# Softmax biases as negated minima, the sink as a column, and 64x64 products dealt over four corners of TensorE

## The reference, cut to what matters

```
# layer 0: 8 dense heads, and 8 window heads (|i-j| <= 128) with a sink
s = where(valid, q @ k.T * scale, NEG)
p = softmax(concatenate([s, sink_col], axis=-1))[..., :-1];  o = p @ v
# layer 1: 8 latent heads, and 8 neighbourhood heads with a bias
s = where(valid, q @ k.T * scale + bias[h], NEG);  o = softmax(s) @ v
# cross attention: 4 heads of 128 (layers 0 and 1), 4 heads of 256 (second block)
k, v = split(m @ w_kv);  q = h @ w_q
o = softmax(q @ k.T * scale) @ v;  out = o @ w_o
# second block, RWKV-7: 8 heads of 64, token by token
sa = S @ -kk;  S = S * w + outer(sa, kk * a) + outer(v, k);  y = S @ r
# second block, GLA: 4 heads, chunks of 64 tokens
att = where(lower triangle, q_dec @ k_inv.T, 0)
o = att @ v + q_dec @ S;  S = exp(dec) * S + k_dec.T @ v
```

## Time and profile before

| | |
|---|---|
| median of 3 runs | 2944.58 us (2944.35 to 2946.43) |
| the profiled execution | 2944.98 us, span 2943.7 us |
| PE busy | 2873.0 us (98%), 14792 matmuls |
| VectorE busy | 1631.0 us (55%) |
| ScalarE busy | 657.2 us (22%) |
| POOL busy | 0.3 us |
| mean granted TensorE clock | 0.995 of full speed |

### The profile page before, as it was taken

One profiled execution on the slowest core, in us unless ns is written; L12 is line 12 of the kernel. 1 busy time (PEld: TensorE's weight loads), 2 busy tenths in 40 slices (PEclk: granted clock), 3 DMA queues, 4 the chain that ended last, 5 costly groups with the idle time before them and its releaser, 6 DMA issues.

```text
span 2943.7 us, 36398 instructions
## 1 busy us (share of the span) xinstructions
PE 2873.0 (98%) x14792; PEld 1974.0 (67%) x14792; DVE 1631.0 (55%) x3300; ACT 657.2 (22%) x1367; POOL 0.3 (0%) x5
## 2 busy tenths in 40 slices
PE   8999999999999999999999999999999999999998
PEld 3557488888544574888885445455554865688886
DVE  5685644453336855566746983445442633666654
ACT  5651310000136513100000021422220102222200
POOL 0000000000000000000000000000000000000000
PEclk9999999999999999999999999999999999999999
DMA  4013122222211131222221111211112331222222
GB/s 145 29 50 101 51 93 86 86 93 101 79 60 50 68 110 65 91 75 86 86 100 65 52 56 58 72 45 45 45 44 80 120 108 43 72 86 87 91 95 79
DMA packets 61942, 224.26 MB, mean 76 GB/s; under 512 B 6992, under 2 KB 7248, under 8 KB 61264
## 3 DMA queue, kind: packets, MB, share of 16 engines
q1 hardware_dynamic: 61776, 221.94, 22.4%
HBM read 219.82 MB, written 2.10 MB: 75 GB/s over the span
## 4 chain that ended last, share of the span: by engine, by line
PE 92%; DVE 7%; issue 1%; DMA 0%; ACT 0%; SPq 0%; DVEq 0%; ACTq 0%
PE ps L1596 28%; PE ps L647 17%; PE ps L1058 15%; PE ps L1046 8%; PE ps L1111 4%; PE ps L1384 2%; PE ps L1357 2%; PE ps L1073 2%; PE ps L1369 2%; PE ps L2278 1%; PE ps L2753 1%; PE ps L2062 1%; PE ps L2083 1%; DVE probs L1487 1%; DVE shaped L1463 1%
## 5 line engine op out<-in xcount | busy, mean ns | idle before, releaser
L1058 PE MATMUL ps<-h,ring 128*128 128x512 f32 x784 | 361.9, 605 | 0.0
L1596 PE MATMUL ps<-h,ring 128*128 128x256 f32 x1136 | 271.0, 382 | 8.5 <-DVE u L1618 4.6
L1058 PEld LDWEIGHTS ps<-h,ring 128*128 128x128 f32 x784 | 142.7, 190 | 158.7 <-issue 152.6
L1596 PEld LDWEIGHTS ps<-h,ring 128*128 128x128 f32 x1136 | 215.9, 191 | 44.0 <-issue 8.7
L1596 PE MATMUL ps<-h_sums,w_sums 128*128 128x256 f32 x1008 | 224.4, 379 | 0.0
L1596 PEld LDWEIGHTS ps<-h_sums,w_sums 128*128 128x128 f32 x1008 | 191.5, 190 | 26.0
L647 PE MATMUL ps<-hid_sums,d_sums 128*128 128x256 f32 x720 | 171.2, 379 | 1.0 <-DVE hid_sums L1555 1.0
L647 PEld LDWEIGHTS ps<-hid_sums,d_sums 128*128 128x128 f32 x720 | 136.6, 190 | 20.2 <-issue 1.8
L1537 DVE TENSOR_TENSOR d_sums<-ring 128x512 f32<-128x512 f32 (+1 forms) x48 | 31.5, 655 | 171.8 <-DMA ring<-stream_dram 146.7
L1369 PEld LDWEIGHTS ps<-constants,probs 128*128 128x128 f32 x560 | 62.7, 141 | 79.2 <-DVE probs L1487 60.0
L1111 PE MATMUL ps<-o_x,ring 128*128 128x512 f32 x256 | 112.2, 593 | 0.0
(11 more groups left out here) (608 smaller groups left out, 4782.2 us busy)
## 6 DMA issues: line engine op xcount, KB each, us to landing
ring<-stream_dram SPq DMA_DIRECT2D x395, 512.0 KB, 3.6
bias<-bias_dram SPq DMA_DIRECT2D x8, 448.0 KB, 4.5
mem<-mem_dram SPq DMA_DIRECT2D x3, 1024.0 KB, 4.8
x<-x_dram SPq DMA_DIRECT2D x4, 512.0 KB, 8.1
out_dram<-x SPq DMA_DIRECT2D x8, 256.0 KB, 2.2
rope_ab<-ropes_dram SPq DMA_DIRECT2D x4, 256.0 KB, 8.3
s_big<-s_big_dram SPq DMA_DIRECT2D x1, 1024.0 KB, 7.0
constants<-constants_dram SPq DMA_DIRECT2D x1, 768.0 KB, 11.3
```

The source lines that it names most:

```text
L1058: mm = pe.matmul(out, w, r, start=(k == 0), stop=(k == len(rhs) - 1))
L1596: mm = pe.matmul(ps[:, bank + at, 0:256], w(k), x(k), start=start and k == 0, stop=k == 3, skip_group_check=not start)
```

## The change

It has five parts.

1. **Window and bias heads.** tensor_tensor_reduce scales by the negated factor and takes a minimum, which is written directly where ScalarE reads its bias; ScalarE then scales by -1. The negation at L1472 goes for them. The negated sink is the first value of that minimum; POOL copies it into one more column of `shaped` (16 copies of 128x2), and the exponential over w+1 columns sums it. L1471, L1436 and L1482 go.
2. **Cross attention, maxima.** The keys are scaled in the copy that takes them out of PSUM, and one tensor_reduce with negation gives the bias.
3. **Cross attention, start.** The last pair's copy and two adds move into the attention's loops: the copy to ScalarE's step 2, the adds to VectorE's steps 2 and 3. TensorE waits for the adds only ahead of the first values. The attention's buffers move to another address (92 or 124 KB).
4. **RWKV.** The scores and the set of L2359 run with c outside and j inside, and two sets (`r_mvp`, `r_tt`) become one loop that alternates them, at the place of the second.
5. **GLA.** The scores alternate two heads. The masked scores of two chunks form a block-diagonal matrix of 128x128 for each head (zeros once by a POOL memset of 128x2048), and one product per two chunks takes the place of two. The mask becomes eight VectorE instructions on 64 partitions. The set starts at time 31.5, not 30.

The diff, cut to what the text speaks of:

```diff
                 for n in range(nh):
                     act.wait_ge(*s['k_p'].at(n + 1))
-                    act.activation(k[:, n, :], ps[:, n % 4, 0:MEM], ACT.Copy).then_inc(*s['k_out'].up())
+                    act.activation(k[:, n, :], ps[:, n % 4, 0:MEM], ACT.Copy, scale=groups[0].scale).then_inc(*s['k_out'].up())
                 for j, b in enumerate(v_banks):
...
                     self.copy_first(act, i, p1[:, :], bank(i))
-                    act.wait_ge(*s['w_p'].at(7 * i + (5 if i else 2)))
-                    act.activation(q[:, 2 * i, lo], ps[:, bank(i), lo], ACT.Copy).then_inc(*s['w_c11'].up())
+                    if i < n_pairs - 1:
+                        act.wait_ge(*s['w_p'].at(7 * i + (5 if i else 2)))
+                    if i < n_pairs - 1:
+                        act.activation(q[:, 2 * i, lo], ps[:, bank(i), lo], ACT.Copy).then_inc(*s['w_c11'].up())
 
             @block.vector
...
+                    if i < n_pairs - 1:
+                        self.combine_last(dve, i, u[:, :], q[:, 2 * i + 1, lo], q[:, 2 * i, hi], bank(i))
 
...
+        def late_act(act):
+            act.wait_ge(*made[0])
+            act.activation(q[:, nh - 2, lo], ps[:, b, lo], ACT.Copy).then_inc(*s['w_c11'].up())
+
+        def late_dve(dve, part):
+            if part == 0:
+                dve.wait_ge(*v_done)
+            dve.wait_ge(*made[part + 1])
+            dst = (q[:, nh - 1, lo], q[:, nh - 2, hi])[part]
+            dve.tensor_tensor(dst, u[:, :], ps[:, b + 2 + part, 0:256], ALU.add).then_inc(*s['w_c'].up())
+        return late_act, late_dve
...
@@ -1340,6 +1359,21 @@
             def width(u):
                 k0, k1 = span(u)
                 return (k1 - k0) * P
+
+            @block.gpsimd
+            def _(pool):
+                done = 0
+                for u, (p, qt) in enumerate(units):
+                    gr = groups[p]
+                    if gr.sink is None:
+                        continue
+                    if not done:
+                        pool.wait_ge(*s['copied'].at(sum(gr.sink is not None for gr in groups)))
+                    if shaped[u - 2]:
+                        pool.wait_ge(*s['exped'].at(u - 1))
+                    w, at = width(u), 2 * sum(gr.sink is not None for gr in groups[:p])
+                    pool.tensor_copy(sb[:, u % 2, :, w], ns[:, at:at + 2]).then_inc(*s['pool'].up())
+                    done += 1
 
             @block.tensor
...
                     if i == 2 and evac is None:
-                        for done in self.q_done:
-                            pe.wait_ge(*done)
+                        pe.wait_ge(*self.q_done[0])
                     if i == 2 and evac and evac.early:
                         pe.wait_ge(*evac.done(False))
                     if 0 <= i - 2 < n:
                         turn(i - 2)
                     p, part = divmod(i - 6, 4)
+                    if late and p == 0 and part == 0:
+                        pe.wait_ge(*self.q_done[1])
                     if evac and p == 0 and part == 0:
                         pe.wait_ge(*evac.done(True))
                     if p >= 0:
...
                         for j in range(g):
                             src = sb[:, i % 2, j, 0:w] if shaped[i] else ps[:, bank(i, j), 0:w]
                             ins = act.activation(pr[:, i % 3, j, 0:w], src, ACT.Exp, bias=stat_of(i, 1, j),
-                                                 scale=1.0 if shaped[i] else gr.scale, accum_out=stat_of(i, 2, j))
+                                                 scale=-1.0 if shaped[i] else 1.0 if gr.folded else gr.scale,
+                                                 accum_out=stat_of(i, 2, j))
                         ins.then_inc(*s['exped'].up())
-                        if gr.sink is not None:
-                            act.activation(stat(i, 5), stat(i, 4), ACT.Exp).then_inc(*s['act'].up())
...
                             a = (6 - 2 * qt) * GRID
                             add = bs[:, gr.bias[j] % 4, a:a + w] if gr.bias else gr.mask(qt)
-                            first = gr.sink[:, j:j + 1] if gr.sink is not None else NEG
-                            dve.tensor_tensor_reduce(sb[:, u % 2, j, 0:w], src, add, gr.scale, first, ALU.add, ALU.max,
-                                                     stat_of(u, 0, j)).then_inc(*s['biased' if j == g - 1 else 'vec'].up())
+                            first = -NEG
+                            if gr.sink is not None:
+                                at = 2 * sum(gr.sink is not None for gr in groups[:p])
+                                first = ns[:, at + j:at + j + 1]
+                            dve.tensor_tensor_reduce(sb[:, u % 2, j, 0:w], src, add, -gr.scale, first, ALU.add, ALU.min,
+                                                     stat_of(u, 1, j)).then_inc(*s['maxed' if j == g - 1 else 'vec'].up())
+                        elif gr.folded:
+                            dve.tensor_reduce(stat_of(u, 1, j), src, AX.X, ALU.max,
+                                              negate=True).then_inc(*s['maxed' if j == g - 1 else 'vec'].up())
                         else:
                             dve.reduce_max(stat_of(u, 0, j), src, AX.X).then_inc(*s['vec'].up())
+                    if shaped[u] or gr.folded:
+                        return
                     dve.wait_ge(*s['vec'].now())
-                    if shaped[u]:
-                        dve.wait_ge(*s['biased'].now())
-                    if gr.sink is not None:
-                        dve.tensor_tensor(stat(u, 4), gr.sink, stat(u, 0), ALU.subtract).then_inc(*s['vec'].up())
-                    dve.tensor_scalar(stat(u, 1), stat(u, 0), -1.0 if shaped[u] else -gr.scale, None,
-                                      ALU.mult).then_inc(*s['maxed'].up())
+                    dve.tensor_scalar(stat(u, 1), stat(u, 0), -gr.scale, None, ALU.mult).then_inc(*s['maxed'].up())
 
                 def scale_rows(u):
-                    nonlocal sinks
                     gr, w = groups[units[u][0]], width(u)
...
                     if evac and i == 2:
                         evac.dve(dve, evac.late)
+                    if late and i in (2, 3):
+                        late[1](dve, i - 2)
                     if 0 <= i - 1 < n:
...
-                                  dv ** -0.5, keys=lambda qt: (0, 2)) for h in range(heads_n)]
-        self.cross_inputs(out, mem, mem_d, g_mem, g_x, k, v, q, groups)
-        self.attention(groups, 0, 4, None, self.residual_fill(self.tiles(o)))
+                                  dv ** -0.5, keys=lambda qt: (0, 2), folded=True) for h in range(heads_n)]
+        late = self.cross_inputs(out, mem, mem_d, g_mem, g_x, k, v, q, groups)
+        self.attention(groups, 92 if nh == 4 else 124, 4, None, self.residual_fill(self.tiles(o)), late=late)
...
+        crossed = [(j, c) for c in range(NC) for j in range(2)]
...
             for w, rhs in enumerate((b.A[:, :], r)):
-                for j, c in chunks:
+                for j, c in crossed:
...
             pe.wait_ge(*s['r_G'].at(5 * i + n))
             pe.wait_ge(*s['r_Tt'].at(6 * i + n))
             if n == 5:
-                blocks(3, other(b.G), other(b.Tt), s['r_tt'], 1)
+                pe.wait_ge(*s['r_vb'].at(i + 1))
+                for j, c in chunks:
+                    vc = vtok[rows(c % 2), c // 2, i * P + 64 * j:i * P + 64 * j + 64]
+                    up = pe.matmul(ps[rows(1 - c % 2), 0, col(j, c)], half(b.mt)(j, c), vc, start=True, stop=True)
+                    mm = pe.matmul(ps[rows(1 - c % 2), 3, col(j, c)], other(b.G)(j, c), other(b.Tt)(j, c), start=True, stop=True)
+                up.then_inc(*s['r_mvp'].up())
+                mm.then_inc(*s['r_tt'].up())
                 continue
             for j, c in chunks:
                 up = pe.matmul(ps[rows(c % 2), 2, col(j, c)], other(b.Tt)(j, c), other(b.G)(j, c), start=True, stop=True)
...
+        for j, c in crossed:
             mm = pe.matmul(ps[rows(j), 4 - 4 * (c % 2), CH * (c // 2):CH * (c // 2) + CH],
                            b.atok[rows(1 - c % 2), c // 2, 64 * j:64 * j + 64], other(b.Tt)(j, c), start=True, stop=True)
         mm.then_inc(*s['r_wp'].up())
...
         pe.wait_ge(*s['s5_glu'].at(4))
-        for h in range(4):
+        for i in range(2):
             for c in range(NC):
                 cc = slice(c * CH, (c + 1) * CH)
-                mm = pe.matmul(ps[rows(c % 2), h, CH * (c // 2):CH * (c // 2) + CH], qk[rows(h % 2), 2 + h // 2, cc],
-                               qk[rows(h % 2), h // 2, cc], start=True, stop=True)
+                for j in range(2):
+                    mm = pe.matmul(ps[rows(c % 2), 2 * i + j, CH * (c // 2):CH * (c // 2) + CH], qk[rows(j), 2 + i, cc],
+                                   qk[rows(j), i, cc], start=True, stop=True)
             mm.then_inc(*s['g_scored'].up())
-        yield 30
-        pe.wait_ge(*s['g_att'].at(4))
+        yield 31.5
+        pe.wait_ge(*s['g_att'].at(8))
```

(17 more changed lines are left out.)

47 lines of the change are left out of this document (23 added, 24 removed).

## The result

The changed kernel takes 2916.15 us (median of 4 runs, 2914.36 to 2917.33), the kernel before 2944.47 (4 runs): the ratio is 0.9904, with a 95% interval of 0.989 to 0.9918. That is 28.3 us less; forecast were 25.1. The profiled execution took 2917.33 us with a span of 2916.0.

A forecast was written before the change was run, and what follows sets the result against it. TensorE was taken as the bound. Window heads 4.0, bias heads 2.4, cross attentions 8.9, RWKV 7.4 and GLA 2.5 sum to 25.2 us, giving 2919.8 for the profiled execution, 2919.5 for the median; range 2912 to 2929.

The forecast's parts named there:

- The bound: Whole kernel: TensorE holds 92% of the chain that ended last, so time counts where it works or waits.
- Window heads: Layer 0's window units: three VectorE instructions go, 0.44 us a unit; 4.0 us gained, 2.0 to 5.1.
- the sign: Window units, profile of the changed kernel: TensorE's idle at 1 us or so, not 5.
- the cap of 5.05: Window units: TensorE's idle of 5.05 us, taken as the most that could be gained.
- Bias heads: Layer 1's bias units: the negation goes; 2.4 us gained, 1.2 to 3.3.
- Cross attentions: Three cross attentions: 6.9 from the starts, 1.2 from the loops, 0.8 from the clock; 8.9 us, 5 to 11.
- The gaps: Each cross attention's start: TensorE's 2.31 us idle ahead of the first transposes goes, three times, 6.9 us.
- The loops: Cross attentions' loops: the negation, 0.07 us from start to start, goes; 0.5, 0.5 and 0.2, sum 1.2 (0.3 to 2.4).
- The clock: Behind the gap in the second and third cross attention: the granted clock may stay up; 0.8 us, 0 to 2.3.
- GLA: GLA: scores 0.40, products 0.5 per pair of chunks, less the longer mask; 2.5 us gained, 1 to 3.
- the signs below 0.3: GLA, profile of the changed kernel: TensorE's wait at the mask below 0.3 us.
- RWKV: RWKV: scores 3.2, merged sets 3.0, L2359 1.2, at the rate of four corners; 7.4 us gained, 5.5 to 8.

The follow-up runs named there:

- exp_first_timed: Changed kernel with ScalarE making unit 2's exponentials ahead of the late copy at each cross attention's start: 2915.30 us, 4 runs; the same kernel's earlier single run exp_first: 2914.20.
- exp_always: Changed kernel with ScalarE making unit i's exponentials ahead of unit i-2's copy at every step of every attention: 2940.60 us, 10 runs, ratio to before 0.9987.

## Why the prediction was right, and where it was off

- **The bound** was read rightly: TensorE. The gain is matmul time where it never waits and waits where it does, and no changed part's gain was given back later (why the rest of the program is 1.0 slower stands at the end of this list).
- **Window heads: 4.0 forecast, 4.04.** TensorE's idle fell from 5.05 to 1.76 (the sign was 1 or so) with no new wait for POOL. That the number is so close is in part luck: 4.0 was picked below the cap of 5.05, which itself leaves out the first units. What happened is that 0.53 a unit went from VectorE's sequence, where I had 0.44, and that it counted only where TensorE waited for VectorE, seven times in these units. Whether VectorE's load or the chain of one unit (maximum, exponentials, scaling) made these waits was argued from loads only; no run separates the two, and that stays open.
- **Bias heads: 2.4 forecast, 1.84.** Right mechanism, size too high. The differences of start show it: they grow in steps of 0.26, seven times in the 16 units (7 x 0.26 = 1.8). The removed negation counts at its full price only in the units ahead of which TensorE waited for VectorE; TensorE's idle of 3.34 was no measure of how often.
- **Cross attentions: 8.9 forecast, 12.3.** The term that was mis-sized. The gaps were right (2.31 gone three times; the late adds are worth 9.1, with 2.2 of that through the clock). For unit 2 I had counted 0.42 of an add on VectorE and left out ScalarE's order, which made its exponentials late: TensorE waited 0.86, 0.87 and 0.44 us, of which exp_first_timed gets 1.7 back. The loops were put at 1.2, and the fold alone is worth 2.2: I took the negation's 0.07 from its own start to the reciprocal's, and left out that it waits for the end of the reduction; from reduction to reciprocal it is 0.19. The clock was put at 0.8 of at most 2.3, on the ground that some of it hides in waits and that the gap alone doesn't decide; filling the gap shows 2.2, hardly any of it hidden. The rest, 12.3 - 6.9 - 2.2 - 2.2 = 1.0, and what made good the new waits ahead of unit 2, are not assigned to one cause.
- **GLA: 2.5 forecast, 3.13.** The scores gave the 0.40. A pair of chunks lost 2.96 - 2.16 = 0.80 us of products (even chunk 1.48 to 1.57, odd 1.48 to 0.59), not 0.5: the odd chunk lost 0.89 where I had counted 0.72, the even one grew by 0.09 where I had 0.18. The mask at 3.60 was beyond my 2.8, since its eight instructions no longer overlap, and TensorE's wait for it was 0.54, where the sum had nothing and the signs below 0.3. With the scores it makes 0.40 + 4 x 0.80 - 0.54 = 3.1.
- **RWKV: 7.4 forecast, 7.35**, set by set at the rates that other sets had shown.
- **What else moved.** The changed kernel is 0.6 ahead from its very start, and loses 0.3 at its end. Between the changed parts the differences of start are flat but for two places, where TensorE waits for VectorE some 3 to 5 us and the granted clock is low around the end of the wait in all kernels: one in layer 1's feed-forward (+1.53 in the changed kernel, -0.06 to +1.62 in the others) and one in S5 (-2.80; -2.82 to +1.62). How long it stays down there differs between traces, though no kernel changes these parts: in the feed-forward the mean over the same 7 us is 0.51 before (1319 to 1326) and 0.76 in the changed kernel (1305 to 1312), and in S5 it is low for some 3 us before (a mean of 0.61 from 1605 to 1609.4) and for some 10 in the changed kernel (0.53 from 1588 to 1599). The one kernel with two traces (exp_first and exp_first_timed) has +0.34 and +0.05 in the feed-forward. That the times of one kernel spread by 3 us for the same reason is likely but not shown. This is also why the steps of a profile tell 0.5 us and the medians don't.

## What to carry to other kernels

An idle gap ahead of a dense stage can cost more than its length: look at the granted clock in the few microseconds behind it, and count that too. Put what only the last consumer needs behind the first softmaxes, and then look at once at which in-order engine makes the next unit late. Price an instruction on a dependent sequence by what stands between its neighbours with and without it, not by the distance of two starts (0.19 here, and not 0.07), and count it only in the units ahead of which the bounding engine waits. Deal small matmuls over all four corners; two gave half the rate in the test, and merging two sets that use opposite corners is as good as reordering one.

## What the runs showed of the hardware

- 32 matmuls of 64x64x64 in fp32 took 3.87 us in one corner, 2.01 in any two, 1.09 in four, with no difference between one bank and two for the row halves. The kernel's own sets on two corners at a time took 1.49 and 1.84.
- After an idle of 2.12 to 2.31 us the granted clock fell to 0.50 for some 3 us in the second and third cross attention and never in the first; with work in that gap it stayed at 1.00. Why not in the first is open. In exp_always it also fell in layer 0's attention, behind a wait of 2.06 us (a mean of 0.72 from 106 to 112).
- POOL copied 128x2 in 0.19 us alone and at 2.75 / 19 = 0.145 in a burst, beside a VectorE at 80%, and the stretch lost 0.04 us with ten copies a unit: no sign that one held up the other at this size.
- A VectorE instruction on 64 partitions cost no less than one on 128: 0.42 to 0.43 us each with 64x256 and with 128x256. Eight of the first took 3.60 us, since they did not overlap; four of the second, which did, took 1.42.
- A negation of 128x1 between a reduction and a reciprocal cost 0.19 us of VectorE's sequence (0.52 against 0.33), though it stood only 0.07 ahead of the reciprocal.
